# The order of the recurrence's instructions on three engines: a planner's durations, tails and due times replaced

## What is computed

```
sa = S @ kk_t
S  = S * w_t - outer(sa, b_t) + outer(v_t, k_t)
y_t = S @ r_t
```

## Time and profile before

| what | value |
|---|---|
| median of three runs | 3450.59 us |
| the profiled execution's own time | 3450.55 us |
| its span, first to last instruction | 3448.5 us |
| TensorE (PE) busy in the span | 3278.7 us (95%) |
| VectorE (DVE) busy | 2078.4 us (60%) |
| ScalarE (ACT) busy | 944.9 us (27%) |
| mean granted TensorE clock | 0.981 |
| the recurrence, 740.0 to 1358.2 us | 618.2 us |

### The profile page before, as it was taken

How to read it: one execution, slowest core, us unless ns; L and a number is a source line. 1 busy time by engine, 2 the same in 40 slices (tenths; PEclk the granted TensorE clock), 3 DMA queues, 4 the chain that set the end, 5 groups by cost and what they waited for, 6 DMA issues and landing times.

```text
span 3448.5 us, 57984 instructions
## 1 busy us (share of the span) xinstructions
PE 3278.7 (95%) x25525; PEld 2065.6 (60%) x25525; DVE 2078.4 (60%) x3695; ACT 944.9 (27%) x1943; POOL 51.9 (2%) x117
## 2 busy tenths in 40 slices
PE   7998899989999998989999999999999999999998
PEld 3446765558888887444444444446566347777853
DVE  3127855547676775655556567669988665434534
ACT  3246741115455554210000100011111403233310
POOL 2000010000000000000000000000000000000000
PEclk9999999989999999999999999999999999999999
DMA  6010003200000002132111116552111112000021
GB/s 248 0 39 18 1 25 122 103 31 19 4 19 3 3 3 79 71 101 73 67 37 49 37 50 245 202 192 88 32 37 61 32 67 62 25 25 25 1 92 67
DMA packets 116863, 211.81 MB, mean 61 GB/s; under 512 B 6083, under 2 KB 67138, under 8 KB 115970
## 3 DMA queue, kind: packets, MB, share of 16 engines
q1 hardware_dynamic: 106818, 175.08, 15.0%
q10 hardware_dynamic: 9792, 33.02, 2.7%
HBM read 181.86 MB, written 26.21 MB: 60 GB/s over the span
## 4 chain that ended last, share of the span: by engine, by line
PE 81%; DVE 11%; ACT 5%; issue 2%; DMA 1%; ACTq 0%; SPq 0%; DVEq 0%
PE psum_all L66 80%; ACT sbuf_all L72 4%; DVE sbuf_all L81 4%; DVE sbuf_all L91 3%; DVE sbuf_all L99 2%; PE psum_all L111 1%; ACT L72 1%; DMA sbuf_all<-in_x 1%; DVE sbuf_all L105 1%; DVE sbuf_all L88 0%; DVE sbuf_all L102 0%; DMA sbuf_all<-in_w_up 0%; DVE sbuf_all L111 0%; DVE sbuf_all L75 0%; ACTq L61 0%
## 5 line engine op out<-in xcount | busy, mean ns | idle before, releaser
L66 PE MATMUL psum_all<-sbuf_all 64*64 64x64 f32 (+10 forms) x24770 | 3196.3, 316 | 140.9 <-ACT sbuf_all L72 73.6
L66 PEld LDWEIGHTS psum_all<-sbuf_all 64*64 64x64 f32 (+4 forms) x24770 | 1982.6, 155 | 1330.0 <-issue 873.1
L72 ACT ACTIVATE sbuf_all<-psum_all 128x256 f32<-128x256 f32 (+5 forms) x925 | 375.1, 426 | 1519.3 <-PE psum_all L66 1302.5
L81 DVE TENSOR_TENSOR sbuf_all<-sbuf_all 128x512 f32<-128x512 f32 (+9 forms) x911 | 607.5, 709 | 233.2 <-ACT sbuf_all L72 125.9
L91 DVE SCALAR_TENSOR_TENSOR sbuf_all<-sbuf_all 128x520 f32<-128x520 f32 (+8 forms) x783 | 581.4, 776 | 16.9
L72 ACT ACTIVATE sbuf_all<-sbuf_all 128x64 f32<-128x64 f32 (+16 forms) x539 | 306.6, 581 | 575.1 <-DVE sbuf_all L87 208.3
L81 DVE TENSOR_TENSOR sbuf_all<-sbuf_all,psum_all 128x512 f32<-128x512 f32 (+3 forms) x188 | 121.1, 646 | 257.4 <-PE psum_all L66 253.4
L72 ACT ACTIVATE sbuf_all<-psum_all,sbuf_all 128x1280 f32<-128x1280 f32 (+5 forms) x212 | 164.8, 784 | 365.0 <-PE psum_all L66 265.6
L105 DVE COPY_PREDICATED sbuf_all<-sbuf_all,psum_all 128x256 f32<-128x256 int32 (+2 forms) x296 | 143.9, 489 | 63.5 <-PE psum_all L66 59.1
L75 DVE COPY sbuf_all<-psum_all 128x512 f32<-128x512 f32 (+8 forms) x93 | 48.8, 532 | 195.8 <-PE psum_all L66 172.4
L87 DVE TENSOR_SCALAR sbuf_all<-sbuf_all 128x256 f32<-128x256 f32 (+9 forms) x151 | 57.6, 418 | 148.3 <-ACT sbuf_all L72 145.1
(11 more groups left out here) (21 smaller groups left out, 177.3 us busy)
## 6 DMA issues: line engine op xcount, KB each, us to landing
sbuf_all<-in_w_down SPq DMA_DIRECT2D x44, 1024.0 KB, 5.0
sbuf_all<-in_w_mod SPq DMA_DIRECT2D x12, 2048.0 KB, 8.0
sbuf_all<-in_w_up SPq DMA_DIRECT2D x22, 1024.0 KB, 7.7
sbuf_all<-in_w_in SPq DMA_DIRECT2D x6, 2048.0 KB, 9.4
sbuf_all<-in_conv_w_in SPq DMA_DIRECT2D x16, 512.0 KB, 5.6
sbuf_all<-in_gla_w_in SPq DMA_DIRECT2D x8, 1024.0 KB, 5.4
hid_spill<-sbuf_all ACTq DMA_DIRECT2D x9, 512.0 KB, 2.6
sbuf_all<-in_x ACTq DMA_DIRECT2D x2, 2048.0 KB, 20.5
```

The source lines that it names most:

```text
L66: return self.e.matmul(out, lhsT, rhs, start=start, stop=stop, skip_group_check=True)
L72: return self.e.activation(out, in_, func, bias=bias, scale=scale, **kw)
L81: return self.e.tensor_tensor(out, a, b, op) if self.e is not None else Unissued()
```

## The change

Three things of the planner are changed, and nothing else in the kernel: every instruction is still there, with the same operands and the same kinds of waits, and only its place in its engine's list is another. The durations of the steps are replaced by others. The time that an engine is held by a step is parted from a `TAIL` behind it (165 ns on TensorE, 35 on VectorE, 30 on ScalarE), after which the result counts as there, and a `HOP` of 40 ns stands for going from one engine to another. And each due time is shifted by a number that depends on the kind of step alone (`LATER`, in ns: negative is earlier). `PACE` becomes 3500.

```diff
-PACE = 4200
+PACE = 3500
+TAIL = {"t": 165, "v": 35, "s": 30}
+HOP = 40
+LATER = {"mask": -4000, "level_de": 22000, "solve": 26000, "level_y": 5000, "gates": -36000, "bonus": -9000, "past": -22000, "products": -10000, "take": 16000, "turned": 18000, "removed": 3000, "key_scale": -2000, "key_inverse": 25000}
...
-            step("t", 870, ("products", gi, pair), *factors, *([("pass", gi - LANES, 3)] if gi >= LANES else []))
-            step("v", 700, ("mask", gi, pair), ("products", gi, pair))
+            step("t", 885, ("products", gi, pair), *factors, *([("pass", gi - LANES, 3)] if gi >= LANES else []))
+            step("v", 655, ("mask", gi, pair), ("products", gi, pair))
...
-    steps, hop = scan_steps(), {"t": 300, "v": 100, "s": 100}
+    steps = scan_steps()
...
-        due[name] = min([end, *(due[x] - hop[e] for x in followers[name])]) - ns
+        due[name] = min([end, *(due[x] - TAIL[e] - HOP * (steps[x][0] != e) for x in followers[name])]) - ns
+    for name in due:
+        due[name] += LATER.get(name[0], 0)
...
-                at = max(at, ends[out] + hop["v"])
+                at = max(at, ends[out] + HOP)
...
-                at = max(at, ends[user] + hop["t"])
+                at = max(at, ends[user] + HOP)
...
-        end = ends[name] = free[e] = start + steps[name][1]
+        free[e] = start + steps[name][1]
+        ends[name] = free[e] + TAIL[e]
...
-                at = max(ends[y] + hop[steps[y][0]] * (steps[y][0] != steps[x][0]) for y in steps[x][2])
+                at = max(ends[y] + HOP * (steps[y][0] != steps[x][0]) for y in steps[x][2])
```

More of the change, by code:

```diff
@@ L1219, in scan_steps @@
         s = 2 * j - 1
-        step("v", 1000, ("keys", j), *halves("removed", s), *halves("rates", s))
+        step("v", 900, ("keys", j), *halves("removed", s), *halves("rates", s))
         step("s", 1270, ("key_squares", j), ("keys", j), *halves("key", s), *halves("bonus_terms", s))
[L1222 to L1226, removed]
+        step("t", 2350, ("key_norms", j), ("key_squares", j))
+        step("s", 190, ("key_roots", j), ("key_norms", j))
+        step("v", 490, ("key_inverse", j), ("key_roots", j))
+        for n, ns in enumerate((640, 640, 390)):
+            step("t", 1000 if n < 2 else 500, ("key_spread", j, n), ("key_inverse", j))
             step("v", ns, ("key_scale", j, n), ("key_spread", j, n))
@@ L1230, in scan_steps @@
         free = [("bonus", s - 1), *halves("beta", s - 1)] if s else []
-        for n, ns in enumerate((860, 860, 430)):
+        for n, ns in enumerate((1060, 1060, 500)):
             step("t", ns, ("gates", s, n), *free)
             for lo in (0, LORA):
-                step("s", 610 if n < 2 else 390, ("gate_out", s, lo, n), ("gates", s, n), *free)
+                step("s", 570 if n < 2 else 360, ("gate_out", s, lo, n), ("gates", s, n), *free)
         for part in range(5):
-            step("v", 690, ("sums", s, part), *(("gate_out", s, 0, n) for n in range(3)), *halves("beta", s - 1),
+            step("v", 585, ("sums", s, part), *(("gate_out", s, 0, n) for n in range(3)), *halves("beta", s - 1),
@@ L1245, in scan_steps @@
             step("s", 700, ("exp_inverse", s, h), ("past", s, h), ("exp_centred", s, h))
             step("s", 700, ("exp_past", s, h), ("past", s, h))
-            step("v", 1400, ("directed", s, h), *(("gate_out", s, LORA, n) for n in range(3)), ("keys", j),
+            step("v", 1440, ("directed", s, h), *(("gate_out", s, LORA, n) for n in range(3)), ("keys", j),
                  ("key_norms", j), *halves("key", s - 1), *halves("bonus_terms", s - 1))
-            step("v", 800, ("rates", s, h), ("directed", s, h), *(("key_scale", j, n) for n in range(3)))
@@ L1250, in scan_steps @@
[L1250 to L1253, removed]
+            step("v", 780, ("rates", s, h), ("directed", s, h), *(("key_scale", j, n) for n in range(3)))
+            step("v", 780, ("received", s, h), ("exp_centred", s, h))
@@ L1254, in scan_steps @@
+            step("v", 780, ("beta", s, h), ("rates", s, h), ("exp_inverse", s, h), *gone(s - 2))
+            step("v", 780, ("key", s, h), ("directed", s, h), ("exp_inverse", s, h), *gone(s - 2))
+            step("v", 780, ("removed", s, h), ("exp_past", s, h), *(("key_scale", j, n) for n in range(3)))
             step("v", 700, ("bonus_terms", s, h), *halves("removed", s), *halves("directed", s))
-        step("t", 1800, ("bonus", s), *halves("bonus_terms", s))
-        step("v", 200, ("bonus_out", s), ("bonus", s))
+        step("t", 1820, ("bonus", s), *halves("bonus_terms", s))
@@ L1257, in scan_steps @@
+        step("v", 150, ("bonus_out", s), ("bonus", s))
     for gi in groups:
```

44 lines of the change are left out of this document (22 added, 22 removed).

## The result

The changed kernel takes 3428.81 us in the median of four runs (3427.2 to 3430.05), beside 3450.21 for the kernel before on the same chip: a ratio of 0.9934, 95% interval 0.9918 to 0.9949. That is 21.4 us faster where 40 were forecast, and 2.8 us above the range. The profiled execution took 3428.11, its span 3426.0.

A forecast was written before the change was run, and what follows sets the result against it. TensorE's 529 us of record starts bound the 618.2 us recurrence, leaving 89 us for order to act on. Waits -33, the rest -4 and half clock -3 gave -40 from 3450.55: 3410 us, range 3397 to 3426.

The forecast's parts named there:

- Opening: TensorE's time not busy before the recurrence's first `products`: 16.4 us, forecast to stay.
- Waits that show: TensorE's visible recurrence waits, 30.0 us in 67 plus 0.22 hidden in each, 45 us: -33, ends -18 and -45.
- The rest: Recurrence waits too short to show and steps wider than priced, 19 us: -4, ends 0 and -14.
- Half clock: Recurrence stretches at clock 0.50, 27.3 us costing 9: one of three goes, -3, ends +5 and -9.
- my own price of 27.5 ns a record: Extra time per TensorE record at half clock, from 16-record steps taking 1.12 us there and 0.68 otherwise.
- the gap between 314 records and 950: In the half-clock stretches TensorE starts 314 records in 27.3 us, where 28.8 ns each would be some 950.
- rival 2: The clock stays up at the recurrence's stream starts: all 9 us come back, some 3404 us; chance 0.16.
- distance and depth: TensorE's list: steps too close fall from 81 to 27; three earlier groups open at 35 of 36 places, before 18.
- Rival 1: Waits move to VectorE and ScalarE, whose masks, turns and `used` come late: only -18, 3432 us; chance 0.14.
- Rival 3: Chunks run bare in the recurrence, 0.69 us lost each: slower once more than 58 of 160 do; chance 0.04.
- the three table loads more: On ScalarE, `key_roots` falls among exponentials: 3 x 1.28 = 3.9 us, left inside the remaining waits.

The follow-up runs named there:

- the filler's run: The changed kernel with 16 matmuls of 64x64 ahead of each `bonus` and of the first two `gates` of streams 1 to 7: 3426.29 us.
- experiment 2: The changed kernel with the `LATER` shift of `gates` at 0 in place of -36000: 3421.58 us, ratio 0.9913.
- the second run of experiment 6: The changed kernel with the rule that `bonus` and `gates` steps start 3.5 us after the one before, sparing the first stream's `gates`: 3409.93 us.
- the two shifts alone: The kernel before with only two `LATER` shifts, `gates` -36 us and `bonus` -9 us: 3428.84 us, ratio 0.9929.
- the two runs of experiment 4: The kernel before with `LATER` added and old durations, hops and `PACE`: 3425.64 us; the changed kernel with `LATER` emptied: 3469.41 us.
- the second run of experiment 4: The changed kernel with `LATER` emptied, keeping new durations, `TAIL`, `HOP` and `PACE`: 3469.41 us, ratio 1.0046.
- experiment 7: The changed kernel with `bonus` and `gates` steps kept 2.5 us apart, not in the first stream: 3406.85 us, ratio 0.9867.
- run 85: Not a run number: 85 counts the table loads of the second run of experiment 6, which took 3409.93 us.
- experiments 1: The changed kernel with each `bonus` or `gates` step held until 3.5 us after the one before, first stream included: 3414.25 us, ratio 0.9888.

## Why the prediction was wrong

The mechanism was right for the waits and wrong for the clock, and the clock's is the only term that came out beyond its ends. By the prediction's own way of counting, from the rows above:

- **Opening.** Forecast to stay at 16.4 us; 29.00 - 12.36 = 16.6, and the rest begins 1.2 us later. Right.
- **Waits that show.** Forecast -33, ends -18 and -45. They went from 45 to 16.2 + 19 x 0.22 = 20 us: -24. 19 waits where 25 or 30 were forecast; but those left are longer, 16.2 us where I had 10 to 15. They are mostly on ScalarE, as said. At -33 the time would have been 9 us lower.
- **The rest.** Forecast -4, ends 0 and -14. What is left of -22.7 after the other terms is -11, or -5 to -8 with the price of half clock that the runs give (below).
- **Half clock: the step that failed.** "I expect one of three stretches to go, since PE will not be busy all through every start of a stream: -3", ends +5 and -9. There are eight stretches with 738 records where there were three with 314. At my own price of 27.5 ns a record that is 20.3 us for 8.6: +12; at the runs' price, +6 to +9. Had it come out at -3, the time would have been 9 to 15 us lower, 3414 to 3420: inside the range.

The price was not what failed. 9 us for 27.3 at half clock is 0.33 for each. To see what the runs give, take the waits that show from the rest of the recurrence, and 0.22 us for each (and from the filler's run its 20.3 us of work). The changed kernel has 546.1 us left with 51.2 at half clock; experiment 2 has 533.7 with none, the second run of experiment 6 533.1 with 3.4, the filler's 534.7 with 13.7, and the two shifts alone 550.0 with 47.8. That is 0.24, 0.27 and 0.30 us for each us at half clock between the changed kernel and the next three, and 0.34 between the last and experiment 2; the two runs of experiment 4, counted in the same way, give 0.38 and 0.37. These are estimates. So of the 20 us by which the changed kernel with the rule is faster (0.0057 of 3452), the clock has some 13 at the 0.27 between these two, and the waits most of the rest.

Why did the step fail? I had read the falls of the clock as places where PE starts little because it *waits*, since in the kernel before long waits and half clock lie together at the starts of streams. So fewer waits had to mean less half clock. (Of the gap between 314 records and 950 that I gave for it, a good part is the lower clock itself: by my own price a record takes 28.8 + 27.5 ns there.) What I had noted under rival 2, that `bonus`, `gates` and `key_norms` still stand at each start, was taken for something that stays, when it is something that the change makes worse: `gates` is due 36 us earlier and `bonus` 9, and so they fall into one run. I had the rows of the new order for it and looked there for distance and depth alone. My upper end, "stretches as many and half as long again", came from no row.

The Trainium skill ("TensorE: Matmul & The Clock Gate", A second HAM failure mode) tells of a kernel in which small idle times between groups of matmuls are frequent enough to bring the clock down and up. By that rule the changed kernel should have had less half clock than before, and the run of experiment 2, with 36 waits, more than the changed kernel. The traces show the reverse of both: the rule fits the second run of experiment 4, and of the change at most the falls with a wait in front.

**The rivals.** Rival 1 (the waits move, 3432) came nearest in time, but it is not what happened: VectorE doesn't hold up PE in mid-stage, and the wait term alone is beyond its -18. Rival 2 (3404) failed in the changed kernel; with the rule it came true, half clock 3.4 us and 3407 to 3410. That these times lie at the forecast's 3410 is luck: they come from another kernel, in which the clock stays up. Rival 3, the bare chunks, isn't there: a bare chunk waits on ScalarE or on L91, and there are 16 such waits in all, where 58 chunks were the point from which it decides. Of the three table loads more (88 for 85) the price can't be told apart: experiment 7 has 88 and experiment 6's second run 85, and the first of these is not slower.

What stays open: how much of the 0.24 to 0.38 us for each us at half clock is PE's own slower work and how much the waits of the steps behind it, since no run fixes the clock and leaves the lists alone. Open too is which trait of these steps it is, the single or few columns, the 32 rows or the fewer starts: the runs move whole steps.

## What to carry to other kernels

When an order is changed, count per place not only the waits but what TensorE is fed between them: a step of one-column or 32-row matmuls is mostly harmless alone (one fall behind a lone `bonus` in experiments 1 and 7) and costs the clock in a run with its like, while the busy share still reads full. Read the granted clock of each stretch beside the idle time, and forecast it from the new order as its own term. And a planner's shifts must be tried together with its spacing rules: two of the thirteen shifts gave all of the gain, until the rule that made the whole set 19 us better took it away from these two.

## What the runs showed of the hardware

- The clock fell from 1.00 to 0.50 at 861.25, 1004.61 and 1226.48 us of the changed kernel after 8 us in which PE had no idle at all, and so it did in all three falls with `LATER` alone. With 17.8 us of idle, 15.6 of it in 36 waits, it stayed at the full clock from 772 to 1326 us (experiment 2).
- Work put in at the right places was free: 704 matmul records, 20.3 us by their spacing, with the time unchanged (3426.29 for 3428.81), because the waits fell from 16.2 to 6.4 us and half clock from 51.2 to 13.7.
- Each us at the half clock cost this stage some 0.24 to 0.38 us (estimates from seven runs).
